# Second tile's first convolution block beside the first tile's LayerNorms, taps packed, convolution LayerNorms two slots earlier

## What is computed

```python
proj = x @ w_in                                   # q, k, v and u (2 x 512 columns)
c_in = u[..., :512] * sigmoid(u[..., 512:])
c = silu(layer_norm(causal_dwconv(c_in, 31 taps)))      # "cln"
attn = window_attention(rope(q), rope(k), v)            # window 128, chunks of 64
h = layer_norm(2**0.25 * x + concat(attn, c) @ w_out)   # "ln1"
up = causal_dwconv(h @ w_up, 3 taps)                    # 2 x 2816 columns
f = (silu(up[..., :2816]) * up[..., 2816:]) @ w_down
ple = sigmoid(h @ w_pg + b_pg) * (p @ w_pe)
y = layer_norm(2**0.25 * h + f + ple)                   # "ln2"
```

## Time and profile before

| | |
|---|---|
| median of three runs | 2437.51 us |
| profiled execution, own time | 2435.67 us |
| its span | 2433.9 us |
| PE busy | 2373.3 us (98%) |
| POOL, DVE, ACT busy | 1601.6, 1466.8, 1277.4 us |
| mean granted TensorE clock | 0.991 of full speed |

### The profile page before, as it was taken

One profiled execution on the slowest core, in us unless ns is written; L12 is line 12 of the kernel. 1 busy time (PEld: TensorE's weight loads), 2 busy tenths in 40 slices (PEclk: granted clock), 3 DMA queues, 4 the chain that ended last, 5 costly groups with the idle time before them and its releaser, 6 DMA issues.

```text
span 2433.9 us, 38834 instructions
## 1 busy us (share of the span) xinstructions
PE 2373.3 (98%) x15081; PEld 2335.4 (96%) x15081; DVE 1466.8 (60%) x2375; ACT 1277.4 (52%) x2083; POOL 1601.6 (66%) x1284
## 2 busy tenths in 40 slices
PE   7999999999999999999999999999999999998997
PEld 7898999999999999999999999999999999998997
DVE  6757883666766267766536766663576665374432
ACT  4556655555444456644444664445465444466653
POOL 8477887765665776566577656557775665777874
PEclk9999999999999999999999999999999999999999
DMA  6244445443333544333344433334443333535443
GB/s 239 97 145 150 165 160 177 163 138 119 120 123 106 168 158 139 123 118 121 110 166 156 147 114 117 123 115 157 153 156 122 116 127 104 174 131 182 165 144 104
DMA packets 119094, 341.54 MB, mean 140 GB/s; under 512 B 15360, under 2 KB 43648, under 8 KB 118912
## 3 DMA queue, kind: packets, MB, share of 16 engines
q1 hardware_dynamic: 98256, 312.89, 38.3%
q10 hardware_dynamic: 20656, 26.17, 3.3%
HBM read 330.12 MB, written 8.99 MB: 139 GB/s over the span
## 4 chain that ended last, share of the span: by engine, by line
PE 86%; DVE 6%; ACT 3%; POOL 2%; DMA 2%; issue 1%; ACTq 0%; DVEq 0%
PE ps L591 28%; PE ps L593 27%; PE ps L592 27%; POOL w_lo L538 2%; DVE sq L1303 1%; DMA w_raw<-in_panels 1%; PE ps L649 1%; ACT w_hi L767 1%; PE ps L680 1%; DVE acc L1240 1%; PE ps L668 1%; PE ps L658 1%; DVE u_out L1168 0%; DVE u_out L1166 0%; PE ps L695 0%
## 5 line engine op out<-in xcount | busy, mean ns | idle before, releaser
L538 POOL TENSOR_TENSOR w_lo<-w_raw,w_hi 128x512 fp32r<-128x512 f32 (+1 forms) x1272 | 1600.6, 1286 | 802.5 <-ACT w_hi L767 796.3
L767 ACT CAST w_hi<-w_raw 128x1024 fp32r<-128x1024 f32 (+2 forms) x635 | 621.5, 981 | 596.4 <-PE ps L593 410.3
L591 PE MATMUL ps<-h_hi,w_hi 128*128 128x386 f32 (+5 forms) x2496 | 815.6, 327 | 7.7 <-DVE f_lo L1181 4.3
L592 PE MATMUL ps<-h_lo,w_hi 128*128 128x386 f32 (+5 forms) x2496 | 807.0, 323 | 0.0
L593 PE MATMUL ps<-h_hi,w_lo 128*128 128x386 f32 (+5 forms) x2496 | 806.9, 323 | 0.0
L591 PEld LDWEIGHTS ps<-h_hi,w_hi 128*128 128x128 f32 x2496 | 473.2, 190 | 15.5 <-issue 8.4
L592 PEld LDWEIGHTS ps<-h_lo,w_hi 128*128 128x128 f32 x2496 | 473.7, 190 | 1.4
L593 PEld LDWEIGHTS ps<-h_hi,w_lo 128*128 128x128 f32 x2496 | 473.9, 190 | 0.0
L591 PE MATMUL ps<-f_hi,w_hi 128*128 128x384 f32 (+2 forms) x1264 | 412.1, 326 | 7.0 <-POOL w_lo L538 4.4
L592 PE MATMUL ps<-f_lo,w_hi 128*128 128x384 f32 (+2 forms) x1264 | 406.5, 322 | 0.0
L593 PE MATMUL ps<-f_hi,w_lo 128*128 128x384 f32 (+2 forms) x1264 | 406.5, 322 | 0.0
(11 more groups left out here) (153 smaller groups left out, 2021.7 us busy)
## 6 DMA issues: line engine op xcount, KB each, us to landing
w_raw<-in_panels SPq DMA_DIRECT2D x540, 512.0 KB, 3.2
w_raw<-in_panels SPq DMA_DIRECT2D x48, 384.0 KB, 3.0
w_raw<-in_panels SPq DMA_DIRECT2D x48, 128.0 KB, 2.3
xres<-in_xT ACTq DMA_DIRECT2D x32, 192.0 KB, 2.7
out_yT<-res ACTq DMA_DIRECT2D x4, 1536.0 KB, 6.4
a_raw<-in_xT ACTq DMA_DIRECT2D x6, 768.0 KB, 6.7
x_raw<-in_xT SPq DMA_DIRECT2D x2, 768.0 KB, 6.7
xres<-in_pT ACTq DMA_DIRECT2D x8, 192.0 KB, 3.3
```

The lines of the kernel that those rows point to most:

```text
L538: ins = pool.tensor_tensor(w_lo[:, n % WS, c], w_raw[:, n % RS, c], w_hi[:, n % WS, c].bitcast(F32), ALU.subtract)
L591: pe.matmul(out, w_hi[:, sl, c], hi, start=first, stop=False)
L592: pe.matmul(out, w_hi[:, sl, c], lo, start=False, stop=False)
L767: act.copy(w_hi[:, n % WS, 0:w], w_raw[:, n % RS, 0:w]).then_inc(w_hi_done, 1)
```

## The change

Four edits in the order of the stages; what is computed is the same. (1) The first convolution block of tile 1 (block 0: 31 taps and the sum) leaves slots 0 to 7 of tile 0. Its `conv_in` copy goes ahead of tile 0's convolution LayerNorm, 5 taps lie between the two halves of `first_norm` (which is cut in `first_norm` and `first_scale`), 16 taps behind the out groups of tile 0 (1, 2, 1, 1, 1, 4, 4, 2), 3 behind the centre of tile 0's ln1, 3, 3 and 2 behind the groups number 1, 2 and 4 of `LATE`; the last of the two is the sum. The `conv_in` of block 1 stands ahead of slot 0. (2) For tile 1 blocks 1 to 3 take slots 0 to 21 (before: four blocks in slots 0 to 24). (3) For tiles 2 to 5 the four blocks take slots 0 to 21 too. (4) Every stage of "cln" for tiles 1 to 5 stands two slots earlier: tree 23, mean and centre 24, square 25, sqtree 26, var and root 27, scale 28, affine and high 29, lo 30. DVE also waits for its own earlier steps before the first tap of a block (`own.wait()`).

```diff
--- before.py
+++ after.py
@@ -85,17 +85,19 @@
                     stage(name, t, u)
         if k == 5 + 4 * (UNITS[t] - 1) + 1:
             stage("att_split", t)
-        taps = {8: (1, 4)}
-        taps.update({n: (0, 4) for n in range(8)})
-        taps.update({n: (1, 7) for n in range(9, 13)})
-        taps.update({n: (2, 4) for n in range(13, 21)})
-        taps.update({n: (3, 8) for n in range(21, 25)})
-        if k in taps:
+        if t == 1:
+
+            counts = {1: [4] * 8, 2: [3, 6, 6, 6, 6, 5], 3: [4, 4, 4, 4, 3, 3, 3, 7]}
+        else:
+            counts = {0: [5, 5, 5, 5, 6, 6], 1: [5, 5, 5, 8, 9], 2: [8, 8, 5, 5, 6], 3: [5, 5, 5, 5, 5, 7]}
+        taps = [(c, n) for c, some in counts.items() for n in some]
+        starts = {n: taps[n + 1][0] for n in range(len(taps) - 1) if taps[n + 1][0] != taps[n][0]}
+        if k < len(taps):
             stage("taps", t, *taps[k])
-        if k in (7, 12, 20):
-            stage("conv_in", t, {7: 1, 12: 2, 20: 3}[k])
-        for name, n in (("tree", 25), ("mean", 26), ("centre", 26), ("square", 27), ("sqtree", 28), ("var", 29),
-                        ("root", 29), ("scale", 30), ("affine", 31), ("high", 31), ("lo", 32)):
+        if k in starts:
+            stage("conv_in", t, starts[k])
+        for name, n in (("tree", 23), ("mean", 24), ("centre", 24), ("square", 25), ("sqtree", 26), ("var", 27),
+                        ("root", 27), ("scale", 28), ("affine", 29), ("high", 29), ("lo", 30)):
             if k == n:
                 stage(name, "cln", t)
 
@@ -138,12 +140,15 @@
     stage("att_split", 0)
     first_taps(1000)
     stage("conv_add", 0, 3)
+    stage("conv_in", 1, 0)
     stage("tree", "cln", 0)
     stage("out_half", 0)
     stage("first_mean", HB - 1, HB)
     stage("out_half", 1)
     stage("out_half", 2)
     stage("first_norm")
+    stage("taps", 1, 0, 5)
+    stage("first_scale")
     stage("out_half", 3)
     stage("out_half", 4)
     stage("lo", "cln", 0)
@@ -153,6 +158,8 @@
             stage("out", i, m)
             if ("ln1", i) in RUNNING and m:
                 stage("run", i, m)
+            if i == 0:
+                stage("taps", 1, 0, (1, 2, 1, 1, 1, 4, 4, 2)[m])
         stage("tree", "ln1", i)
         fill = [("d", i - 1, 2, m) for m in range(KB)] if i else [("in", 1, g) for g in LATE]
         if 1 <= i < LAST:
@@ -176,6 +183,7 @@
             one = {0: (0, "var", "root", "scale"), 1: (1, "affine"), 2: ("high", 2), 3: ("lo", 3), 4: (4,)}
             for name in ("mean", "centre", "square"):
                 stage(name, "ln1", 0)
+            stage("taps", 1, 0, 3)
         for n, g in enumerate(fill):
             stage(*g)
             for name in one.get(n, ()):
@@ -183,6 +191,8 @@
                     stage("rope", 1, LATE[name])
                     continue
                 stage(name, "ln1", i)
+            if i == 0 and n in (1, 2, 4):
+                stage("taps", 1, 0, {1: 3, 2: 3, 4: 2}[n])
             for name in two.get(n, ()):
                 stage(name, "ln2", i - 1)
             if 1 <= i < LAST and n in (3, 5):
@@ -195,7 +205,7 @@
         slots += [[("u", i, 2 * j), ("u", i, 2 * j + 1)] for j in range(17, FB)]
         slots += [[("pg", i, m), ("pe", i, m)] for m in range(KB)]
         if i < LAST:
-            stage("conv_in", i + 1, 0)
+            stage("conv_in", i + 1, 0 if i else 1)
         split = None
         for k, two_groups in enumerate(slots):
             for g in two_groups:
@@ -1227,6 +1237,7 @@
                 both = (res[:, 2 * c, :], res[:, 2 * c + 1, :]) if t == 0 else (acc[:, 0, :], acc[:, 1, :])
                 first = len(marks)
                 if first == 0:
+                    own.wait()
                     dve.wait_ge(conv_in, n + 1)
                 for k in range(first, first + count):
                     if k == CONV_K:
@@ -1376,6 +1387,9 @@
                 for c in range(HB):
                     z = a_raw[1][:, c, 0:w]
                     dve.tensor_tensor(z, z, ps[:, AUX, 0:w], ALU.subtract).then_inc(centred, 1)
+
+            def first_scale():
+                w = WIDTH[0]
                 dve.wait_ge(std_done, 1)
                 std = ps[:, AUX + 1, 0:w]
                 own.step(dve.reciprocal(std, std))
@@ -1464,6 +1478,8 @@
                     rest(*e[1:])
                 elif what == "first_norm":
                     first_norm()
+                elif what == "first_scale":
+                    first_scale()
                 elif what == "last_norm":
                     last_norm()
```

## The result

| | before | changed |
|---|---|---|
| median of 22 runs each | 2435.93 us | 2439.13 us |
| profiled execution, span | 2433.9 us | 2440.0 us |
| ratio of the times | | 1.0015 (95%: 1.0009 to 1.0021) |

What follows compares the result with a forecast made beforehand. PE was taken as the bound, busy 2373.3 of 2433.9 us. Terms 0 + 0.7 - 3.4 + 1.2 + 0 + 0 = -1.5 us gave 2434.2 us for the profiled execution, 2436.0 for the median; range 2429.5 to 2442.5.

Steps and rivals of the forecast that it cites:

- slots 8 to 20: Tile 0: fewer taps on DVE shorten PE's waits ahead of d part 1 and keep the clock up behind; -3.4 us.
- Block 0 beside the LayerNorms: Ahead of slot 0: block 0's taps fit DVE's pauses, so PE gains and loses nothing; 0 us.
- The last taps and the copy: Behind the LATE groups: last tap and block 1's copy delay the first u_out and lengthen PE's divide wait; +0.7 us.
- The sqtree in slot 26: Tile 0: sqtree behind the split for pe ends late, so PE waits at slot 27's end; +1.2 us, bounds 0 and +2.0.
- The pg window: Tile 0's pg groups: old 7.9 us loss replaced by 4.1 wait at third group, 1.7 clock, 2 at end; 0 us.
- Rival B: Third pg group: PE waits over 4 us, low clock twice as long, window 5 us longer; +6.6 us, 2444; chance 0.13.
- Rival C: Slots 8 to 20: ACT holds DVE, only 0.25 us goes, clock still falls; +1.7 us, 2439.2; chance 0.17.
- The tiles behind: Tiles 1 to 4: PE has no waits these stages set, so nothing is won; 0 us, up to +1.

Runs made afterwards that it cites:

- e1: Changed kernel with only the convolution LayerNorm's stages put back in their old slots, two later; 2436.36 us, ratio 1.0000 to the kernel before.
- e7: Changed kernel with block 0's last tap ahead of the last rope and the copy of block 1's input right behind it; ratio 1.0008 to the kernel before.
- e6: Changed kernel with the convolution's LayerNorm finished ahead of the last two u slots and the split for pe in slot 28; ratio 0.9992 to the kernel before.
- e4: Changed kernel with tile 1's block 0 back in tile 0's slots, all 128 units in 22 slots; 2453.2 us, ratio 1.0068 to the kernel before.
- e3: Changed kernel with ACT's copy of block 1's input behind slot 0's u groups and product, not ahead of them; ratio 1.0020 to the kernel before.
- e5: Changed kernel with the split for pe in slot 25, affine and high in slot 30, lo in slot 31; ratio 1.0003 to the kernel before.
- e9: Changed kernel with the edits of e6 and e7, plus the next tile's residual loads moved from slot 33 to 29; 2432.68 us, ratio 0.9985 to the kernel before.
- e2: Changed kernel with the split for pe moved from slot 26 to slot 25; ratio 1.0007 to the kernel before.

## Why the prediction was wrong

Two terms of the sum failed. The gain of 3.4 us in slots 8 to 20 did not come, since most of the lead that DVE was to win is lost at slot 12; and the sqtree's +1.2 us was +4.1 in the profile, since its length was taken from another place and no low clock was counted behind its wait. By the ratios, the edits on the taps (forecast +0.7 - 3.4 = -2.7 us) gave 0.0, with 2.2 us either way (e1), and the LayerNorm's stages (forecast +1.2 + 0) gave +3.7.

**Block 0 beside the LayerNorms: right.** PE's waits over 0.2 us from 100 us to slot 0 sum to 4.75 us, 4.74 before, and one by one they are the same within 0.01 us.

**The last taps and the copy: right, +0.56 for +0.7.** The copy waited 3.24 us for the tap and ran at 169.71, to compare with the earlier trace rows; in e7, with the same taps in another order, the wait for `divide` was 1.87 us again and slots 0 to 8 took 66.23: the order was the cause, not DVE's load.

```profile
169.71 0.51 ACT L848 COPY ps<-g_in 128x414 f32<-128x414 f32 x1 [3.24 <-DVE acc L1251]
170.25 0.22 ACT L851 COPY g_in<-g_in 128x30 f32<-128x30 f32 x1
170.37 0.56 ACT L871 ACTIVATE u_out<-ps,par 128x256 f32<-128x256 f32 x1
```

**Slots 8 to 20: the step that failed in the gain, -0.66 for -3.4 in the profile.** "I take 1.75 us" of DVE's lead was too much: the waits ahead of d part 1, 2.31 and 0.25 us, fell only by 0.84, to 1.72 (1.26 to 1.95 in the experiments with these taps). DVE did fewer taps but then stood 2.13 us waiting for PE's last d group of slot 12, where I had allowed one or two of the six taps to be lost:

```profile
259.32 0.42 DVE L1209 SCALAR_TENSOR_TENSOR res<-h_hi,ps 128x256 f32<-128x256 f32 x1 [2.13 <-PE ps L603]
```

Four of the six taps, those of slots 8 to 11, lie ahead of this wait. Before the change DVE did not wait there, but it was already level with PE: its next instruction (the low part of `res`) began 0.38 us ahead of slot 13, and now 0.46 us ahead of it (259.77 against 260.23). So four taps won 0.08 us, and two were left to win, one in slot 12 and one in slots 13 to 19: 1.1 us by the earlier trace rows, an estimate, where the profiles with these taps show 0.6 to 1.3.

The other half of that term was 1.6 us of clock. In the changed kernel's profile the clock did stay up behind slot 20 (1.00 in slots 21 to 24, for 0.93 before in the same stage), and that stage fell from 24.59 to 23.45 us. But this is no certain gain: in e1, with the same edits, the clock fell there and the stage took 24.59. And slots 9 to 12 took 1.49 us more in the profile with the clock low in their first microseconds, but 26.78 to 26.82 in all ten experiments. So the +1.49 is this execution's. What the taps give is 0.8 to 1.5 us in slots 13 to 20 against the one profile of before, and in eight of ten profiles with these edits (not in e1 and e6, where the clock fell) 0.8 to 1.1 in slots 21 to 24.

**The sqtree in slot 26: the mechanism right, the size outside my bounds; the second step that failed.** "I take +1.2, bounds 0 and +2.0": the stage grew by 4.09 us, of which the wait is 2.46. I had carried over its length of 2.85 us from slot 28; behind the split it took 3.58.

```profile
346.65 1.95 DVE L1198 TENSOR_TENSOR f_lo<-xres,f_hi 128x256 fp32r<-128x256 f32 x2 [0.20 <-ACT f_hi L906]
348.53 3.58 DVE L1314 TENSOR_TENSOR sq<-sq 128x768 f32<-128x768 f32 x2
```

That is two instructions, of 768 and 384 elements. The second took 1.50 to 1.53 us in all of these profiles; the first took 2.04 in the changed kernel and in e4, 0.95 in e3 and e7, and 1.28 before. What differs is POOL's instruction beside it. In the changed kernel POOL's had begun 0.10 us ahead:

```profile
348.43 1.33 POOL L548 TENSOR_TENSOR w_lo<-w_raw,w_hi 128x512 fp32r<-128x512 f32 x1
...
348.53 2.04 DVE L1314 TENSOR_TENSOR sq<-sq 128x768 f32<-128x768 f32 x1
```

In e3 DVE's began 0.04 us ahead, and it was POOL's that took longer:

```profile
347.74 0.95 DVE L1317 TENSOR_TENSOR sq<-sq 128x768 f32<-128x768 f32 x1
...
347.78 2.03 POOL L551 TENSOR_TENSOR w_lo<-w_raw,w_hi 128x512 fp32r<-128x512 f32 x1 [0.24 <-ACT w_hi L780]
```

e4 is as the changed kernel, e7 as e3 (its two began within 0.01 us of each other). Before the change POOL's began 0.82 us ahead, so that less of it was left, and DVE's took 1.28 us. The Trainium skill ("SBUF — State Buffer", SBUF: two separate sides) has a rule for that: where a VectorE instruction has two inputs in SBUF and a GpSimd one reads SBUF, the pair of ports is locked for a whole instruction by whichever of the two starts first, and the other is blocked. The trace agrees, with 1.09 us between the two cases. PE's wait was 2.46 us in the changed kernel and e4, with a low clock behind it and 33.95 and 34.10 us for the stage, and 1.38 and 1.39 in e3 and e7, without one and with 31.45 and 31.48 us. So my +1.2 was near what one of the two cases gives (+1.6), and far from the other. The rest of the 4.09 us is clock: 0.95 in the window, about 1.7 us, which I had left out behind this wait though I had priced it behind the other two.

**The pg window: the wait right, 4.25 us for 4.1; the sum, +0.49 for 0, in part by luck.** The bank of the last u group was the next thing late, e5 and e6 show it from both sides. But the 28.8 us that I took for the window without losses is too little: with a clock of 1.00 PE was busy for 30.30 us there in e6 and 30.25 in e9. So 6.5 us were lost before, not 7.9, and of these the clock had some 1.1 (31.43 us busy for 30.3), not 3.3; part of its fall lay in PE's own wait. The changed kernel lost 4.25 us at the third group, some 1.2 by the clock (1.7 in the sum) and 1.50 at the end (2 in the sum). In the other profiles with this wait the window took 37.50 (e2), 37.81 (e7), 39.22 (e4) and 39.96 us (e3), for 36.77 before and 37.00 in e1: the trade is even at best. I had put this as a term and not as the verdict on the edit: an edit that moves a wait of 5 us to a new one of 4 us can only gain what the other terms leave.

**The sum.** Of the LayerNorm's +3.7 us the sqtree has 1.9 by the ratios (e2), with wide intervals; how the rest is shared is not shown. I had the places of all the waits; two sizes were wrong, both toward the gain, and the forecast's own bounds (from -1.0 in the slots and +2.0 for the sqtree) would have given +1.7. Rival B's mechanism (the third pg group with a low clock) held in part, without its 5 us in that window. Rival C's outcome (little won in slots 8 to 20) held, but not its mechanism: DVE waited for PE, not for ACT. The median of 2436.0 was reckoned from three runs of the kernel before at 2437.51; from its 22 runs, 2435.93, the same sum would have given 2434.4. The tiles behind did not change, as forecast.

## What to carry to other kernels

When a stage is moved earlier in an order written by hand, look at each engine for what is queued directly behind its new place, and for the buffer that this releases: here affine and high stood, from 370.72 us on, ahead of the instructions that empty a bank which PE wanted at 373.42 and got at 377.67. Moved three to four slots earlier instead of two, with the split behind it, the same LayerNorm took 5.6 us less than in the changed kernel (e6); against the kernel before, its 1.9 us are barely told from nothing. Ask also whether the engine that is relieved has, before the place where the time is wanted, a wait for the engine that it should run ahead of: what was won ahead of such a wait is lost there. Take the length of an instruction that runs beside another engine's from the place where it will stand, and where it can be blocked by that engine, give it both ends of what the profile shows (0.95 and 2.04 us here).

## What the runs showed that I had not expected

**A low clock can be free.** Before the change PE waited 0.30 us ahead of d part 0, in the changed kernel 1.83; I first read that as a new wait. But in the stretch ahead of it the clock was 0.87 before and 0.97 (low only at its end, behind the wait) in the changed kernel. The window 220 to 233 us of the kernel before:

```profile
220.00:233.00 13.00, 10.84 (x77) 9.94 (x75) 10.94 (x22) 7.95 (x16) 8.83 (x7) 0.87 0.47 161
```

The same window of e7, where the clock stayed at 1.00 and PE waited 1.86 us:

```profile
220.00:233.00 13.00, 10.19 (x84) 9.26 (x82) 10.24 (x20) 7.94 (x15) 9.02 (x7) 1.00 0.49 161
```

Slots 0 to 8 took 66.23 us in both. The matmuls were slow or PE waited, for the same low part from DVE; in these profiles only a fall of the clock where PE is the bound cost time. Where the stages are the same, the falls come and go behind the same waits: the second wait for `divide`, 1.86 us, had one behind it in the kernel before and in e1, none in the changed kernel and in e7; the wait ahead of d part 0, 1.83 us, had one in the changed kernel and none in e9. Ahead of d part 1, waits of 1.26 to 1.79 us had none behind them, and those of 1.93 (e6), 1.95 (e1) and 2.31 us (before) had one.
